# Last attention: inverse denominators carried to the feature rows by small transfers instead of TensorE transposes

## The reference, cut to what matters

```python
qf = concatenate([q[..., :C_NOPE], q_rope])        # 64 + 32 features per head
kf = concatenate([kv[..., :C_NOPE], k_rope])       # the rotary key is shared by all heads
v  = kv[..., C_NOPE:]
scale = (C_NOPE + C_ROPE) ** -0.5
s  = einsum("bqhd,bkhd->bhqk", qb, kf) * scale
pr = softmax(s, axis=-1)                           # over 256 keys
o  = einsum("bhqk,bkhd->bqhd", pr, v)
return o.reshape(bsz, seq, 1024) @ w_out
```

## Time and profile before

| | us |
|---|---|
| median of 3 runs | 843.82 (843.4 to 845.42) |
| profiled execution, its own time | 842.86 |
| its span | 841.1 |
| PE busy | 830.9 (99%) |
| DVE busy | 580.7 (69%) |
| ACT busy | 437.1 (52%) |
| POOL busy | 58.2 (7%) |

### The profile page before, as it was taken

The page is one execution under the profiler, slowest core; times in us unless marked ns, Lnnn a source line. Parts: engine busy times, 40 slices in busy tenths (PEclk is TensorE's granted clock), DMA queues, the critical chain, the costliest instruction groups (busy, mean ns, idle before and its releaser), DMA issues.

```text
span 841.1 us, 12750 instructions
## 1 busy us (share of the span) xinstructions
PE 830.9 (99%) x5022; PEld 726.9 (86%) x5022; DVE 580.7 (69%) x621; ACT 437.1 (52%) x598; POOL 58.2 (7%) x121
## 2 busy tenths in 40 slices
PE   8999999999999999999999999999999999999996
PEld 8977988888888799989888888999867988888885
DVE  5897656665668689886866666677787576666663
ACT  6675544344435688665544444446664554444431
POOL 2200000000000213410000000013000000000000
PEclk9999999999999999999999999999999999999999
DMA  8744364645564595365766665444515276655511
GB/s 331 301 144 152 126 201 154 226 168 198 174 226 154 168 284 193 109 199 146 249 199 199 199 199 192 144 143 137 203 53 175 77 250 199 199 184 183 186 46 51
DMA packets 92360, 149.79 MB, mean 178 GB/s; under 512 B 4540, under 2 KB 71628, under 8 KB 91808
## 3 DMA queue, kind: packets, MB, share of 16 engines
q1 hardware_dynamic: 90608, 143.90, 50.9%
q0 software_dynamic: 1424, 5.07, 1.9%
q10 hardware_dynamic: 288, 0.27, 0.1%
HBM read 148.15 MB, written 1.06 MB: 177 GB/s over the span
## 4 chain that ended last, share of the span: by engine, by line
PE 92%; DVE 4%; ACT 2%; DMA 1%; issue 1%; SPq 0%; DVEq 0%; POOLq 0%; POOL 0%; ACTq 0%
PE bank L1960 20%; PE bank L1961 20%; PE bank L1962 20%; PE bank L1988 17%; PE bank L1991 9%; PE bank L2044 1%; ACT arena L1171 1%; DMA w_raw<-laid_swa_w_in_blocks 1%; DVE w_lo L1224 1%; DVE arena L1895 1%; PE bank L2358 1%; PE bank L2150 1%; PE bank L2169 1%; PE bank L2658 0%; ACT w_hi L699 0%
## 5 line engine op out<-in xcount | busy, mean ns | idle before, releaser
L1224 DVE TENSOR_TENSOR w_lo<-w_raw,w_hi 128x2048 fp32r<-128x2048 f32 (+2 forms) x126 | 282.6, 2249 | 64.5 <-ACT w_hi L699 64.5
L699 ACT ACTIVATE w_hi<-w_raw 128x2048 fp32r<-128x2048 f32 (+1 forms) x128 | 239.5, 1878 | 54.2 <-PE bank L1962 40.4
L1988 PE MATMUL bank<-xT,w_hi 128*128 128x512 f32 x640 | 159.4, 391 | 0.0
L1988 PEld LDWEIGHTS bank<-xT,w_hi 128*128 128x128 f32 x640 | 117.1, 188 | 22.3
L1960 PE MATMUL bank<-w_hi,ff_hi 128*128 128x512 f32 x344 | 134.5, 391 | 0.0
L1961 PE MATMUL bank<-w_lo,ff_hi 128*128 128x512 f32 x344 | 134.3, 390 | 0.0
L1962 PE MATMUL bank<-w_hi,ff_lo 128*128 128x512 f32 x344 | 133.9, 389 | 0.0
L1960 PE MATMUL bank<-xT,w_hi 128*128 128x256 f32 (+1 forms) x428 | 122.8, 287 | 0.0
L1962 PE MATMUL bank<-xT,w_lo 128*128 128x256 f32 (+1 forms) x428 | 121.0, 283 | 0.0
L1961 PE MATMUL bank<-xT,w_hi 128*128 128x256 f32 (+1 forms) x428 | 121.0, 283 | 0.0
L1991 PEld LDWEIGHTS bank<-xT,w_lo 128*128 128x128 f32 x640 | 87.3, 190 | 6.2
(11 more groups left out here) (269 smaller groups left out, 912.6 us busy)
## 6 DMA issues: line engine op xcount, KB each, us to landing
w_raw<-in_ffn_w SPq DMA_DIRECT2D x64, 1024.0 KB, 5.3
w_raw<-in_ffn_w_gate_up SPq DMA_DIRECT2D x22, 1024.0 KB, 5.1
w_raw<-in_ab_w_in SPq DMA_DIRECT2D x12, 1024.0 KB, 6.9
w_raw<-in_ffn_w_down SPq DMA_DIRECT2D x11, 1024.0 KB, 5.1
w_raw<-in_swa_w_out SPq DMA_DIRECT2D x4, 1024.0 KB, 8.1
w_raw<-in_ab_w_out SPq DMA_DIRECT2D x4, 1024.0 KB, 4.9
w_raw<-in_c_w_out SPq DMA_DIRECT2D x4, 1024.0 KB, 6.2
w_raw<-laid_swa_w_in_blocks SPq DMA_DIRECT2D x3, 1024.0 KB, 13.3
```

The costliest lines, as they stand in the source:

```text
L699: act.activation(view(w_hi, ch), view(w_raw, ch), ACT.Copy).then_inc(S["hi_done"], 1)
L1224: dve.tensor_tensor(view(w_lo, ch), view(w_raw, ch), view(w_hi, ch).bitcast(F32), ALU.subtract).then_inc(S["lo_done"], 1)
L1988: pe.matmul(bank[b + f], hi[:, k, f * P:(f + 1) * P], xT[:, k].rearrange("p s t c -> p (s t c)"), start=k == 0, stop=False)
```

## The change

POOL's spreading, PE's transposes and ACT's copy of bank 1 go. In their place DVE writes a quad's 8 reciprocals per query (4 heads by 2 token tiles) into a 32-column buffer and transposes it in 32x32 blocks into `c_rows` (`dve.transpose`). Of each of the 4 partition blocks the 8 useful rows are 128 bytes long; two blocks are stored to a tensor in device memory by ACT's queue (`store_rows`), two by POOL's queue. POOL waits for all four and then loads them back twice, each time 2 KB repeated over 64 partitions, into `c_R`, which now has two buffers. DVE's `output` waits for these loads.

Bank 1 is free by that. PE transposes the even head of pair 2n (n = 1 to 3) into bank 1 and its odd head into bank 2, and ACT, not DVE, copies banks 1 and 2 (`transposed_even`). `output_low` of a quad moves one round later on DVE.

```diff
@@ POOL
             for n in range(QUADS):
-                pool.wait_ge(S["c_rden_ready"], n + 1)
-                if n:
-                    pool.wait_ge(S["c_R_psum"], n)
-                pool.tensor_copy(c_rdx, c_rden[:, :, 4 * n:4 * n + 4].unsqueeze(3).broadcast_to([P, NT, 4, CV])).then_inc(S["c_rdx_ready"], 1)
+                pool.wait_ge(S["c_rows_ready"], n + 1)
+                for a in (2, 3):
+                    pool.dma_start(shares[n, :, a * 32:a * 32 + 32], c_rows[a * 32:a * 32 + 4 * NT, n % 2]).then_inc(S["c_rows_put"], 16)
+                pool.wait_ge(S["c_rows_put"], 32 * (n + 1))
+                pool.wait_ge(S["c_rows_stored"], 32 * (n + 1))
+                if n >= 2:
+                    pool.wait_ge(S["c_of_ready"], n - 1)
+                for e in range(2):
+                    src = shares[n, 2 * NT * e:2 * NT * (e + 1)].rearrange("(a c) q -> a (c q)", a=1).broadcast_to([CV, 2 * SEQ])
+                    pool.dma_start(c_R[n % 2][CV * e:CV * (e + 1), :], src).then_inc(S["c_R_loaded"], 16)
@@ ACT
-            def denominators(n):
-
-                act.wait_ge(S["c_R_psum"], n + 1)
-                if n:
-                    act.wait_ge(S["c_of_ready"], n)
-                act.activation(c_R, bank[1][:], ACT.Copy).then_inc(S["c_R_ready"], 1)
+            def transposed_even(p):
+                act.wait_ge(S["c_pt_psum"], p + 1)
+                act.wait_ge(S["c_o_psum"], p - 1)
+                act.activation(c_pT[:, 0].rearrange("p e k c -> p e (k c)"), psum[:, 1:3], ACT.Copy).then_inc(S["c_pt_ready"], 1)
...
+            def store_rows(n):
+                act.wait_ge(S["c_rows_ready"], n + 1)
+                for a in (0, 1):
+                    act.dma_start(shares[n, :, a * 32:a * 32 + 32], c_rows[a * 32:a * 32 + 4 * NT, n % 2]).then_inc(S["c_rows_stored"], 16)
             probabilities(0)
             probabilities(1)
+            store_rows(0)
             query_tiles(3)
             high_half(o[1], 0)
             high_half(o[1], 1)
             for n in range(1, QUADS):
                 probabilities(2 * n)
                 probabilities(2 * n + 1)
-                denominators(n - 1)
+                store_rows(n)
+                transposed_even(2 * n)
                 output_high(n - 1)
             split[0] = o[1].index + 1
-            denominators(QUADS - 1)
@@ DVE
             def reciprocals(n):
                 dve.wait_ge(S["c_probs"], 8 * (n + 1))
-                hs = slice(4 * n, 4 * n + 4)
-                dve.reciprocal(c_rden[:, :, hs], c_sum[:, :, hs]).then_inc(S["c_rden_ready"], 1)
+                if n >= 2:
+                    dve.wait_ge(S["c_R_loaded"], 32 * (n - 1))
+                den = c_den[:, n % 2]
+                step(dve.reciprocal(den[:, 0:4 * NT].rearrange("p (e j t) -> p e j t", e=2, j=2),
+                                    c_sum[:, :, 4 * n:4 * n + 4].rearrange("p t (j e) -> p e j t", e=2)))
+                dve.transpose(c_rows[:, n % 2], den).then_inc(S["c_rows_ready"], 1)
...
             def output(n):
                 dve.wait_ge(S["c_o_psum"], 2 * n + 2)
-                dve.wait_ge(S["c_R_ready"], n + 1)
+                dve.wait_ge(S["c_R_loaded"], 32 * (n + 1))
...
                 transposed_p(2 * n - 1)
+                if n > 1:
+                    output_low(n - 2)
                 if n < 3:
                     low_half(o[1], n - 1)
                 output(n - 1)
-                transposed_p(2 * n)
-                output_low(n - 1)
@@ PE
                 transposed_p(2 * n - 1)
                 outputs(2 * n - 2)
-                denominators(n - 1)
+                pe.wait_ge(S["c_rope_ready"], QUADS)
+                pe.wait_ge(S["c_pt_ready"], 2 * n - 1)
+                transposed_head(2 * n, 0, 1)
                 outputs(2 * n - 1)
-                transposed_p(2 * n)
+                transposed_head(2 * n, 1, 2)
...
             transposed_p(PAIRS - 1)
-            denominators(QUADS - 1)
             outputs(PAIRS - 2)
             outputs(PAIRS - 1)
```

More of the change, by code:

```diff
@@ L181, in build @@
         rows = nc.dram_tensor("decay_rows", (AH, 2 * SEQ), F32, kind="Internal").ap()
+        shares = nc.dram_tensor("share_rows", (QUADS, 2 * NT * 2, P), F32, kind="Internal").ap()
         pos_i = sb("pos_i", [P, NT], I32)
@@ L296, in build @@
         c_sum = take(P, NT, CH)
-        c_rden = take(P, NT, CH)
+        c_den = take(P, 2, P // 4)
+        c_rows = take(P, 2, P // 4)
         used[0] = pT_at
@@ L302, in build @@
         c_csT = take(P, 2 * NT * P).rearrange("p (w t j a i) -> p w t j a i", w=2, t=NT, j=4, a=2)
-        c_R = x_norm[:, 0, 0:512]
+        c_R = (x_norm[:, 0, 0:512], x_norm[:, 1, 0:512])
         c_of = x_norm[:, 0, 512:1024]
-        c_rdx = x_norm[:, 1, 0:512].rearrange("p (t h e) -> p t h e", t=NT, h=4)
         psum = ctx.enter_context(nc.psum_tensor("bank", [P, 8, 512], F32))
@@ L328, in build @@
             "c_vh c_vl c_v_psum c_v_ready c_k_psum c_k_ready c_qn_psum c_qn_ready c_rope_ready "
-            "c_krT_psum c_krT_ready c_scores c_nmax c_probs c_pt_psum c_pt_ready c_rden_ready c_rdx_ready c_R_psum c_R_ready "
+            "c_krT_psum c_krT_ready c_scores c_nmax c_probs c_pt_psum c_pt_ready c_rows_ready c_rows_stored c_R_loaded c_rows_put "
             "c_o_psum c_of_ready c_oh c_ol "
@@ L1912, in output @@
                 dve.wait_ge(S["c_o_psum"], 2 * n + 2)
-                dve.wait_ge(S["c_R_ready"], n + 1)
+                dve.wait_ge(S["c_R_loaded"], 32 * (n + 1))
                 if n:
                     dve.wait_ge(S["c_ol"], n)
-                dve.tensor_tensor(c_of, bank[0][:], c_R, ALU.mult).then_inc(S["c_of_ready"], 1)
+                dve.tensor_tensor(c_of, bank[0][:], c_R[n % 2], ALU.mult).then_inc(S["c_of_ready"], 1)
             def output_low(n):
@@ L1922, in output_low @@
                                   ALU.subtract).then_inc(S["c_ol"], 1)
+            step(dve.memset(c_den, 1.0))
             maxima(0)
@@ L1941, in _ @@
             transposed_p(PAIRS - 1)
+            output_low(QUADS - 2)
             output(QUADS - 1)
@@ L2619, in scores, with transposed_head @@
                 last.then_inc(S["c_scores"], 1)
+            def transposed_head(p, e, b):
+                pe.wait_ge(S["c_probs"], 4 * p + 2 * (e + 1))
+                for k in range(2):
+                    for t in range(NT):
+                        at = (NT * k + t) * P
+                        last = pe.transpose(bank[b][:, at:at + P], c_p[:, p % 2, e, t * SEQ + k * P:t * SEQ + (k + 1) * P], ident[:])
+                if e:
+                    last.then_inc(S["c_pt_psum"], 1)
             def transposed_p(p):
-                pe.wait_ge(S["c_probs"], 4 * (p + 1))
                 if p:
@@ L2627, in transposed_p @@
                 for e in range(2):
[L2628 to L2644, removed]
-                                            c_rdx[:, t, 2 * j:2 * j + 2, :].rearrange("p h e -> p (h e)"), ident[:])
-                last.then_inc(S["c_R_psum"], 1)
+                    transposed_head(p, e, 2 + e)
             def outputs(p):
```

## The result

| | before | changed |
|---|---|---|
| median, 9 runs each | 843.45 us (842.81 to 845.42) | 847.03 us (846.71 to 851.6) |
| ratio to before | | 1.0051, 95% interval 1.0041 to 1.0060 |
| profiled execution, time and span | 842.86, 841.1 | 846.78, 845.0 |
| PE busy | 830.9 | 829.3 |
| DVE busy | 580.7 | 578.6 |

A forecast was written before the change was run, and what follows sets the result against it. PE's own queue bounds the attention's 8.0 us rounds, with a 7.3 us chain through ACT right under. Worked delays and gains move the projection's resumption from 635.58 to 638.15: +2.6 on 842.86, plus 0.96, gives 846.4; range 843.4 to 850.0.

The forecast's parts named there:

- The wait ahead of pair 7's transposes: End of attention: PE wants these transposes at 633.5, gets them at 634.8 because ACT's copy waits for quad 3's rows.
- Trips: Way through memory, from a quad's rows ready to `c_R` loaded: 6.3 us, but 6.8 for quad 0, 7.1 for quad 2.
- Issues on ACT: Each store issue on ACT's queue holds ACT 0.45 us; if nearly free (0.1), round 0's delay would be 0.7 less.
- The largest term: Round 0: ACT waits for quad 0's rows, so exponentials of quad 1 come 2.6 us late, ropes of quad 2 2.2.
- Denominators off PE: PE's attention rounds lose 0.76 us of work: gain 0.5 to 0.7 in each of two rounds, 0.4 at the end.
- the chain of 7.3: Ropes, scores, maxima and ACT's exponentials (3.5 + 3.8 us a round) set the round once PE needs about 7.1.
- the bank frees no further work of PE: Attention, bank 1 freed from denominators: no gain for PE, since transposes are as many as before.
- The rival of a long trip: Memory trips of 8.5 to 9 us, or 7.9 throughout, bound the rounds: +4.5 to +8 us, 849 to 852; chance 0.20.
- The rival of the clock: Idle PE near 611 to 613 and 633.5 to 634.8 drops to 1.2 GHz: another +1 to +3 us; chance 0.04.
- From the profiled execution to the median: Whole program: the median of the runs shown lies 0.96 us above the profiled execution, so 845.4 becomes 846.4.
- rival 2: Trip of 5.6 us or below gives +1.4, with issues of 0.1 also +0.4: 844.2 to 845.2; chance 0.18.
- rival 3: Round 0: ACT is not held, only PE's shorter queue counts; projection resumes near 634.0, -1.6 us, 842.2; chance 0.06.

The follow-up runs named there:

- swap0: Changed kernel, but in round 0 ACT issues its two stores behind the query tiles and the chunk's two halves; ratio to the kernel before 1.0044.
- swapn: Changed kernel, but in rounds 1 to 3 ACT copies the transposes of pair 2n before issuing quad n's stores; ratio to the kernel before 1.0011.
- held_load: Changed kernel, but SP holds the second 1 MB feed-forward weight load until quad 2's reciprocals are back from memory; ratio to the kernel before 1.0013.
- before_none: Kernel before without POOL's spreading, PE's denominator transposes and ACT's copy of bank 1, `c_R` set to one; ratio to the unedited kernel before 1.0000.

## Why the prediction was right, and where its steps were off

It forecast +2.6 us, 846.4, within 843.4 to 850.0, slower by over 0.3% with a chance of one half; measured 847.03 and 1.0051. The mechanism was right: ACT held by rows, rows late by the trip, PE waiting for ACT's copy ahead of pair 7. That the total came within 0.6 us is in part luck, since errors in both directions cancel (below). The worked rounds can be checked one by one, with 0.66 us taken off for the later first ropes:

| step | forecast | measured, less 0.66 |
|---|---|---|
| rows of quad 0 | 608.3 | 608.28 |
| exponentials of quad 1 | 611.85 | 611.60 |
| ropes of quads 2, 3 | 615.7, 623.05 | 615.40, 622.80 |
| rows of quads 1, 2, 3 | 616.3, 624.35, 632.6 | 616.16, 623.83, 633.68 |
| transposes of pair 7 | 634.8 | 635.51 |
| projection resumes | 638.15 | 638.93 |

The wait ahead of pair 7's transposes was 1.3 us in the forecast (633.5 to 634.8) and measured 2.49.

- *Trips.* Forecast 6.8, 6.3, 7.1; measured from rows to output 6.83, at most 6.63, 8.80. The one that is off is quad 2's, by 1.7 us, and it is on the path: the term that was mis-sized. For a store beside a load I had 3.0 us to land, from four small transfers between buffers; behind the 1 MB load the stores took 4.3 to 4.4, and POOL went on 5.19 after their first issue. I took a busy stretch as a fixed surcharge; here the store lands just behind the load instead. Rows of quad 2 were 0.5 us earlier than forecast, which hid part of it. A load of 128 KB lands in 2.7 us (median of eight, 2.7 to 3.0), where I took 3.0. By the Trainium skill ("DMA: Bandwidth & Descriptors", section "Anatomy of one DMA") it would be 2.3 by estimate: a little short.
- *Issues on ACT* take 0.85 for the first pair and 0.62 for later ones, not 0.9: 0.05 us less hold in round 0, 0.28 less in each later one.
- *The largest term was named wrongly.* I called ACT's hold in round 0 (2.2 us on the ropes) the largest term with nothing to cover it. The hold is real and of that size, but swap0 gives back only 0.42: quad 0's trip, 6.8 us, holds DVE and then ACT to nearly the same point. The gap ahead of pair 7's transposes is the large one, 2.5 us, as swapn and held_load show. The two aren't terms of a sum: together they give back 3.60.
- *"Denominators off PE", a gain of 0.5 to 0.7 a round:* the size fits (0.60 in the second round), and the bound named for it, the chain of 7.3, is what holds the round (7.40). But before_none shows that taking them off gives nothing by itself. The step that failed is "the bank frees no further work of PE": the traces read as if the bank makes the gain, by letting transposes run while DVE copies (not separated from the copy's move to ACT).
- *The rival of a long trip* (0.20) happened for one quad of four. *The rival of the clock* (0.04) happened too, on top of the forecast: in the profiled execution of the changed kernel the clock stayed at 1.00, in the second profile it fell. The attention lost 3.35 us by the first trace, the medians 3.58, and the ratio of the means 3.5 to 5.1; the means hold the runs at 848 to 851.6, and falls of the clock fit them, though only one was profiled.
- *From the profiled execution to the median* I added 0.96 us, from three runs. The nine runs of before lie 0.59 above it and those of the changed kernel 0.25 above theirs. So the base was too high and the loss (2.6 against 3.58) too small, and the two errors offset each other.
- *Two slips in the working.* The end is called some 0.7 us earlier for a trip of 5.6, but 1.2 earlier (+1.4 for +2.6) in rival 2. And 0.26 + 0.18 + half of rival 3 is 0.47 by itself, not 0.43. The forecast rests on neither.

## What to carry to other kernels

A wait on a transfer belongs behind everything in that engine's queue that others need, above all where the engine only issues the transfer: here two changes of order, with the same work, turned 1.0051 into 0.9994. Before an instruction group on the bounding engine is counted as gain, look at what it covers: the next instruction may be waiting for a copy anyway. A round trip through memory of 6 to 7 us that is started and awaited in the same chain sets a round of its own; start it before the previous one is awaited, and check which bulk load it meets: what counts is when that load lands, so a store issued earlier into the same load gains nothing.

## What the runs showed of the hardware

- A store of 1 KB to device memory (8 rows of 128 bytes, POOL's queue) landed in 1.5 to 1.6 us with no load under way (quads 1 and 3 of the changed kernel; the 8 KB store of the earlier trace rows took 1.7), so the short rows alone show no cost here. Issued 0.6 to 2.4 us behind a 1 MB load that took 5.2 to 5.5, it landed in 5.0 down to 3.1 us, at most 0.7 behind the load. Moving the load moved the delay to another quad (held_load), and with all four stores on ACT's queue POOL still went on 5.4 us behind the rows. Whether stores of longer rows would wait as well was not tried.
- An issue on ACT's queue held ACT 0.27 to 0.54 us, one on POOL's held POOL 0.51 to 0.55.
- A 32x32 block transpose of 128x32 float32 on DVE took 0.21 us.
- PE idle for 2.4 to 2.8 us kept 2.4 GHz in two executions (2.37 in swap0, 2.49 in the changed kernel) and fell to 1.2 GHz in two others (2.61 and 2.83), for about 3 and 7 us. The prediction had given this a chance of 0.04.
